# Two hybrid layers walk one written order of steps: chain steps between projection halves, attention in head pairs between inverse levels

## What is computed

```python
h = rmsnorm(x, norm_w)
proj = h @ w_in                      # 1024 x 3752
y_mla  = mla_mixer(m_cq, m_ckv, m_kr, ...) * silu(m_gate)      # 4 heads, causal attention
y_gdn  = gdn_mixer(g_q, g_k, g_v, g_z, g_b, g_a, ...)          # conv, l2norm, gated delta rule
y_moba = moba_mixer(c_q, c_k, c_v, t5_table) * silu(c_gate)    # 4 heads, causal attention
return x + concatenate([y_mla, y_gdn, y_moba]) @ w_out
```

## Time and profile before

| | us |
|---|---|
| median of 3 runs | 2756.01 (2755.51 to 2759.61) |
| the profiled execution, its own time | 2757.31 |
| its span | 2755.5 |
| PE, DVE, ACT, POOL busy in the span | 2437.0, 1251.7, 951.5, 24.8 |
| granted TensorE clock, mean | 0.931 |
| first product of the first hybrid layer | 2130.8 |
| first output product of that layer | 2404.7 |
| the same two of the second layer | 2440.7 and 2711.5 |

### The profile page before, as it was taken

How to read it: one execution, slowest core, us unless ns; L and a number is a source line. 1 busy time by engine, 2 the same in 40 slices (tenths; PEclk the granted TensorE clock), 3 DMA queues, 4 the chain that set the end, 5 groups by cost and what they waited for, 6 DMA issues and landing times.

```text
span 2755.5 us, 40784 instructions
## 1 busy us (share of the span) xinstructions
PE 2437.0 (88%) x15118; PEld 2029.1 (74%) x15118; DVE 1251.7 (45%) x1770; ACT 951.5 (35%) x1299; POOL 24.8 (1%) x24
## 2 busy tenths in 40 slices
PE   4999998899879999979999977988997977798776
PEld 3788886777658888858888756767996965688565
DVE  2433235555653223363323363555546555456453
ACT  2333223443443332233332232345544332143312
POOL 0000000000000000000000000000000000000000
PEclk8999999999989999989999988999999977898787
DMA  8453643222125536432345315113564420044000
GB/s 276 152 165 95 187 141 99 89 81 92 47 61 168 171 102 184 124 90 77 91 135 176 107 47 133 62 62 92 160 185 132 151 79 1 1 141 154 1 1 16
DMA packets 396730, 298.03 MB, mean 108 GB/s; under 512 B 10814, under 2 KB 358596, under 8 KB 396484
## 3 DMA queue, kind: packets, MB, share of 16 engines
q1 hardware_dynamic: 364372, 231.46, 28.9%
q10 hardware_dynamic: 32240, 65.01, 6.8%
HBM read 295.38 MB, written 1.06 MB: 108 GB/s over the span
## 4 chain that ended last, share of the span: by engine, by line
PE 74%; DVE 12%; issue 7%; ACT 4%; SPq 1%; DMA 1%; POOL 1%; DVEq 0%; ACTq 0%; POOLq 0%
PE banks L764 21%; PE banks L765 20%; PE banks L766 20%; DVE wl L1813 3%; ACT wh L1362 3%; PE banks L694 2%; PE banks L745 2%; DVE yT L1779 2%; DVE probn L1792 1%; PE banks L730 1%; PE banks L915 1%; PE banks L738 1%; POOL stat L1696 1%; PE banks L936 1%; DVE big L2206 1%
## 5 line engine op out<-in xcount | busy, mean ns | idle before, releaser
L764 PE MATMUL banks<-uR,wh 128*128 128x512 f32 (+1 forms) x2368 | 831.0, 351 | 60.5 <-DVE uR L1779 42.0
L765 PE MATMUL banks<-uR,wh 128*128 128x512 f32 (+1 forms) x2368 | 819.6, 346 | 0.0
L766 PE MATMUL banks<-uR,wl 128*128 128x512 f32 (+1 forms) x2368 | 818.7, 346 | 0.0
L1813 DVE TENSOR_TENSOR wl<-wraw,wh 128x2048 fp32r<-128x2048 f32 (+1 forms) x224 | 488.6, 2181 | 498.3 <-ACTq L1310 496.7
L1362 ACT ACTIVATE wh<-wraw 128x2048 fp32r<-128x2048 f32 (+1 forms) x224 | 409.1, 1826 | 461.3 <-PE banks L766 414.1
L764 PEld LDWEIGHTS banks<-uR,wh 128*128 128x128 f32 x2368 | 457.8, 193 | 127.5 <-issue 74.4
L766 PEld LDWEIGHTS banks<-uR,wl 128*128 128x128 f32 x2368 | 456.7, 193 | 53.1
L765 PEld LDWEIGHTS banks<-uR,wh 128*128 128x128 f32 x2368 | 457.9, 193 | 49.9 <-issue 0.2
L764 PE MATMUL banks<-gR,wh 128*128 128x512 f32 (+1 forms) x704 | 256.8, 365 | 8.9 <-DVEq L1723 8.9
L765 PE MATMUL banks<-gR,wh 128*128 128x512 f32 (+1 forms) x704 | 255.2, 363 | 0.0
L766 PE MATMUL banks<-gR,wl 128*128 128x512 f32 (+1 forms) x704 | 255.1, 362 | 0.0
(11 more groups left out here) (273 smaller groups left out, 2378.6 us busy)
## 6 DMA issues: line engine op xcount, KB each, us to landing
wraw<-in_ffn_w_in SPq DMA_DIRECT2D x176, 512.0 KB, 5.1
ada_buf<-in_ada_w ACTq DMA_DIRECT2D x27, 2048.0 KB, 8.9
wraw<-in_w_in SPq DMA_DIRECT2D x56, 512.0 KB, 4.7
wraw<-in_ffn_w_out SPq DMA_DIRECT2D x64, 384.0 KB, 4.1
wraw<-in_ffn_w_out SPq DMA_DIRECT2D x64, 320.0 KB, 3.6
wraw<-in_da_w_in SPq DMA_DIRECT2D x24, 512.0 KB, 4.6
wraw<-in_na_w_in SPq DMA_DIRECT2D x24, 512.0 KB, 4.6
yT<-in_ada_w ACTq DMA_DIRECT2D x4, 2048.0 KB, 8.2
```

The costliest lines, as they stand in the source:

```text
L764: mm(o, a[0], b[0], start=first, stop=False)
L765: mm(o, a[0], b[1], start=False, stop=False)
L766: return mm(o, a[1], b[0], start=False, stop=last)
L1813: do(V.tensor_tensor(wl[:, s, 0:n], wraw[:, s, 0:n], wh[:, s, 0:n].bitcast(F32), ALU.subtract), w_lo)
```

## The change

`HY_ORDER` is one list of steps that PE, ACT, DVE and POOL all walk in a hybrid layer. Each engine takes from it the steps that concern it, and does them in that order. A block is now two half steps ("W", n, 0) and ("W", n, 1), and chain steps stand between them. The blocks' order in time is 3, 4, 5, 6, 7, 8, 11, 2, 9, 10, 15, 0, 1, 12, 13, 14 (the weights are loaded in that order). Banks of PSUM are given out by `hy_products`: banks 0 and 1 to blocks, a ring of three (2, 3, 4) to the chain, another of three (5, 6, 7) to `mla`; before, blocks and chain turned over four. `mla` and `moba` attention items are pairs of heads (8 items instead of 16), with one maximum over both heads, and their steps stand between the levels of the inverse and the products of the states. Convolution is now two chunks behind each of blocks 3 to 8. Tiles of the chain (`Xm`, `XT`, `Ym`, `LmT`) lie in the unused half of the activation buffer, diagonals alternate between two buffers, and one semaphore per kind of result takes the place of the two counters. The first output block is cut into four parts.

The letters: St statistics, Di and Fd diagonals and spreads, Sc scaling of q and k, S silu and squares, Ge and Gb gates, T transposes of k and v, Cu and Cb cumulative decays, De decays, KK and QK products, Dv vectors, TL and TY transposes of L, Xi first X, L and P the levels, F the products of the states, Fs and Fc statistics and scaling of the output, Ms, Md, Me, Mq, Mk, Mv, Mr, Mp the parts of `mla`, As scores, At transposes and Av values of an item, U and V halves of the output's input, O output blocks.

```diff
+            first = [*w(3), *w(4), ("W", 5, 0), ("S", 0), ("W", 5, 1), ("W", 6, 0), ("St", 0), ("W", 6, 1), ("W", 7, 0), ("S", 1),
+                     ("Di", 0, 0), ("W", 7, 1), ("St", 1), ("W", 8, 0), ("Sc", 0, 0), ("Di", 0, 1), ("W", 8, 1), *w(11), ("Sc", 0, 1),
+                     ("Di", 1, 0), ("W", 2, 0), ("S", 2), ("Ge",), ("Sc", 1, 0), ("Di", 1, 1), ("W", 2, 1), ("Sc", 1, 1), ("Gb",),
+                     ("W", 9, 0), ("T", 4, 0), ("T", 4, 1), ("W", 9, 1), ("T", 8, 0), ("T", 8, 1), ("Cu",), ("W", 10, 0),
+                     ("Cb", 0), ("Cb", 1), ("W", 10, 1), ("W", 15, 0), ("KK", 0), ("W", 15, 1), ("De",), ("KK", 1), ("W", 0, 0), ("QK", 0),
+                     ("Dv",), ("W", 0, 1), ("QK", 1), ("TL", 0), ("W", 1, 0), ("TL", 1), ("TY", 0), ("W", 1, 1), ("TY", 1),
+                     ("Xi", 0), ("W", 12, 0), ("Ms",), ("Xi", 1), ("W", 12, 1), ("Md", 0)]
+            fill = [[("Me", 0), ("Md", 1), ("W", 13, 0)], [("Me", 1), ("W", 13, 1)],
+                    [("Mq", 0), ("W", 14, 0)], [("Mq", 1), ("Mk", 0)],
+                    [("W", 14, 1), ("Mk", 1)], [("Mr", 0), ("Mv", 0)],
+                    [("Mr", 1), ("Mv", 1)], [("Mp",)]]
+            n = 8
+
+            def item(i):
+                return [("As", i + 1)] * (i + 1 < n) + [("At", i)] + [("Av", i - 1)] * (i > 0)
+
+            fill += [[("As", 0)], *[item(i) for i in range(n)], [("Av", n - 1), ("U", 6)], [("V", 6)], [("O", 0, 0, 0)]]
+            levels = [[[("L", m, 0), ("L", m, 1)], [("P", m, 0), ("P", m, 1)]] for m in range(1, LEVELS)]
+            chain = [x for level in levels for x in level]
+            chain += [[("F", i)] for i in range(1, 7)] + [[("Fs",)], [("Fd", 0)], [("Fc", 0), ("Fd", 1)], [("Fc", 1)]]
+            order = first
+            for x in range(max(len(chain), len(fill))):
+                order = order + (chain[x] if x < len(chain) else []) + (fill[x] if x < len(fill) else [])
...
+                        rest_next()
+                        if 3 <= n <= 8:
+                            convolve(2 * (n - 3))
+                            convolve(2 * (n - 3) + 1)
+                            dve.sem_inc(conv_done, 1)
...
+                    elif kind == "As":
+                        i = at_[0]
+                        b, nk = i % 2, items[i]["nk"]
+                        product(hs_full, *tok, 1)
+                        do(V.reduce_max(negm[:, b, 1, :], banks[:, 0:2, 0:nk], AX.X, negate=True), peak_ready)
+                    elif kind == "At":
+                        i = at_[0]
+                        b, nk = i % 2, items[i]["nk"]
+                        dve.wait_ge(hexp_ready, 8 * l + i + 1)
+                        do(V.reciprocal(rsum[:, b, 1, :], rsum[:, b, 0, :]))
+                        for j in range(2):
+                            x = hprob[:, b, j, 0:nk]
+                            do(V.tensor_scalar(x, x, rsum[:, b, 1, j:j + 1], None, ALU.mult), *([hprob_ready] if j else []))
```

More of the change, by code:

```diff
@@ L410, in moba_items @@
+            for p in range(2):
                 for t in range(2):
                     nk = (t + 1) * P
[L412 to L419, removed]
@@ new lines, in hybrid, with take, four @@
+                items = list(hy_items())
+                w = {}
+                def take(*key):
+                    b, before, _ = HP[(l, *key)]
+                    if before:
+                        pe.wait_ge(hb_free[b], before)
+                    return psum[b]
+                def four(key, pairs):
+                    o = take(*key)
+                    for h in range(GH):
+                        parts = pairs(h)
+                        for k, (a, b) in enumerate(parts):
+                            ins = mm(o[:, h * P:h * P + P], a, b, start=(k == 0), stop=(k == len(parts) - 1))
+                    ins.then_inc(hg_full, 1)
@@ L1599, in hybrid, with product @@
-                for k in (2, 4):
-                    step_v()
-                    A_(uR[:, 0, k:k + 2, CTX:T], yc[:, k:k + 2, :], ACT.Copy).then_inc(uh_ready, 1)
-                for b in range(4):
-                    gemm.up()
-                    lead_next()
+                act.wait_ge(v_hyb, tl["vh"].up())
+                items = list(hy_items())
+                def product(full_sem, *key):
+                    b, _, full = HP[(l, *key)]
+                    act.wait_ge(full_sem, full)
+                    return psum[b], hb_free[b]
@@ L2066, in hybrid, with product, by_head, two @@
                 do(V.memset(convin[:, :, 0:PAD], 0.0))
+                items = list(hy_items())
+                def product(full_sem, *key):
+                    b, _, full = HP[(l, *key)]
+                    dve.wait_ge(full_sem, full)
+                    return psum[b], hb_free[b]
+                def by_head(o):
+                    return o.rearrange("p (a n) -> p a n", n=P)
+                def two(o):
+                    return o.rearrange("p (a n) -> p a n", a=2)
                 def convolve(k):
@@ new lines, in statistics, with spread_out @@
+                def statistics(o, free, means):
+                    for a, e, at_, inv, eps in means:
+                        do(V.tensor_scalar(stat[:, 0, a:e], o[:, at_:at_ + e - a], inv, eps, ALU.mult, ALU.add))
+                    dve.sem_inc(free, 1)
+                    dve.sem_inc(var_ready, 1)
+                    tl["root"].up()
+                def spread_out(tok):
+                    a, nt, d = hy_diag(tok)
+                    dve.wait_ge(root_ready, tl["root"].now())
+                    do(V.tensor_tensor(d[:, 0:nt * P].rearrange("p (a n) -> p a n", n=P), rep(ident, nt),
+                                       wide(stat[:, 1, a:a + nt], P), ALU.mult), hd_ready)
```

1196 lines of the change are left out of this document (636 added, 560 removed).

## The result

The changed kernel takes 2769.93 us (median of 5 runs, 2769.43 to 2771.51); its ratio to the kernel before is 1.0048, 95% interval 1.0034 to 1.0063. It is slower by 0.5%, about 14 us. 2729 was predicted, with 2685 to 2760 as the range, so the time lies outside the range and on the other side of the old one. The profiled execution took 2770.25, its span is 2768.5.

What follows compares the result with a forecast made beforehand. PE's work in the block stage and the round trips to DVE or ACT behind it bound the kernel. Per layer 182 + 34 + 18 + 13.5 = 247.5 us; with tails 27.3 us saved in all, so 2729 us, range 2685 to 2760.

Steps and rivals of the forecast that it cites:

- The clock: Time PE loses at the lower clock: start, block 11 and four holes of 4 us and more, 13.5 us per layer.
- holes of 0.3 to 0.9 us: Short PE holes in the inverse were said to cost no clock, since it has them and 0.96.
- The rest of the sum: Per layer besides clock: 182 us PE work, 34 us block-part waits, 18 us inverse-part waits.
- Rival 2: Holes keep PE at the lower clock through the inverse part: +19 us per layer, 2767 us; 12 in 100.
- The list of waits: PE's waits at named steps, walked: 34 us in the block part, 18 us in the inverse part.
- PE's work: PE's products over a hybrid layer, nearly kept and summed at full clock: 182 us.
- The tail: From last state product to first output product: 3.5 us less than the 14.7 us, per layer.
- Everything else in the kernel stays: Outside the hybrid layers' stretches and tails no time was expected to change.
- What would show it: Profile signs: named DVE-released holes, first layer 247 us, inverse-part clock 0.85 or more; wrong if block part under 135 us.
- 0.75 or less: Granted clock in the inverse part that would show the prediction wrong and Rival 2 right.

Runs made afterwards that it cites:

- experiment 7: Changed kernel, on DVE alone: convolution behind q and k diagonals, scaling ahead of next maximum, `mla` diagonals ahead of ("Xi", 1) and block 12's low half; 2701.11 us.
- experiment 4: Changed kernel, on DVE alone: convolution chunks behind the diagonals of q and k, most of these also ahead of a low half; 2749.25 us.
- experiment 5: Changed kernel, on DVE alone: scaling of each attention item ahead of the next item's maximum; 2738.92 us.
- swap_conv_md: Same run as experiment 7: the DVE moves of experiment 4 and experiment 5 plus the `mla` diagonals moved earlier, against the changed kernel; 2701.11 us.
- experiment 6: The DVE moves of experiment 4 and experiment 5 together, against the changed kernel; 2716.09 us.

## Why the prediction was wrong

**The step that failed is "The clock"**, and in it the term for the item part. The prediction took 13.5 us per layer for the start, block 11 and four long holes, and nothing for the seven holes of 1.6 to 1.8 us among the items. It went by holes of 0.3 to 0.9 us that leave 0.96, and stretched that to twice the length. Measured, PE is busy 12.8 us (first layer) and 7.7 us (second) more in the item part than the same instructions take at the full clock (experiment 7), where the sum has nothing.

The rest of the sum held better. Split by its own terms it gives some 147 us for the block part, 54 for the levels and 47 for the item part (P of level 5 and level 6 7.6, states 7, items 20, holes 12), as an estimate. They are 151.0, 55.8 and 59.7 in the first layer, so 13 of the 19.0 us missed lie in the item part, and 154.4, 55.8 and 55.9 in the second (266.1 for 247.5), so 9 of 18.6. In the block part of the first layer work and clock make some 113 by the sum, and PE is busy 113.2.

**Rival 2 came nearest**: it named this place, "the holes keep PE at the lower clock through the inverse part", and gave 2767 for 2769.93. It got 12 in 100. Its size was right partly by chance: it spread a clock of 0.75 over levels and items, where both together have 0.83 (0.93 and 0.74), and idle time and the block part make up the rest. Its premise, that gaps like the items' stood in today's attention, isn't what that stage shows. PE waited there 4.55 us once and 1.67 us once, and otherwise at most 0.7. Two stretches of it, in the kernel before:

```profile
2272.70:2294.30 21.60, 18.10 (x81) 10.62 (x80) 12.97 (x43) 7.77 (x27) 0.00 (x0) 0.96 0.01 2
2294.34:2311.36 17.02, 16.42 (x46) 8.63 (x46) 6.30 (x21) 4.03 (x14) 0.00 (x0) 0.51 0.00 0
```

The first holds the hole of 1.67 us and has 0.96. The second begins behind holes of 0.64 and 0.68 us, has 0.6 us of idle time in all, and stands at the lower level. So the mean of 0.71 was a warning, but not about long gaps, and "holes of 0.3 to 0.9 us cost nothing" was not safe either. The Trainium skill, "TensorE: Matmul & The Clock Gate", Part 1, says that the array is slow unless activity releases it. The runs agree in direction, since work that computes nothing made the kernel 13.6 us faster; the 17 us in which PE was busy at the lower level aren't explained by it.

**The list of waits held.** Predicted, then measured in the first layer: ("Di", 0, 0) 6.2 and 7.77; ("Di", 0, 1) 2.2 and 3.48; ("Di", 1, 0) 8 and 8.39; ("T", 4, 0) 2.2 and 2.49; ("TY", 0) 3.1 and 4.91; ("Md", 0) 6.5 and 5.68; the items 1.6 to 1.8 and 1.66 to 1.91. ("St", 0) was 4.3 and is 2.38. The mechanism, work that is not urgent ahead in DVE's queue, is shown by experiments 4, 5 and 7, each of which changes that queue alone. ("As", 0) was 1.6 and is 2.20. No wait that wasn't named is over 5 us; 1.48 us for ACT in the item part was not on the list (2.40 in the second layer).

**PE's work** of 182 us at full clock can't be read off directly. swap_conv_md is busy 198.6 us in the same three stretches, two of them at 0.85 and 0.97, so 182 can be right, and no run shows it.

**The tail** was taken at 3.5 us less per layer. From the last state product to the end of the output it is 35.7 for 40.6 and 35.6 for 39.2: 4.9 and 3.6 less. Right.

**"Everything else in the kernel stays"** was wrong by 4 us: the first layer starts 1.1 later (2131.90 for 2130.80), and the stretches between the layers and behind the last take 2.3 and 0.8 more.

**What would show it**: the block part over 135 us (151.0) and the holes at the named steps came. "0.75 or less" in the inverse part, the sign that it was wrong, came for the items of the first layer (0.74), not for those of the second (0.85) and not for levels and items together (0.83).

## What to carry to other kernels

When several engines walk one list, its order must be asked for on each engine apart: PE wants the next item's scores between this item's scores and its transposes, and DVE wants this item's scaling ahead of the next item's maximum. One list can't say both, and the swap on DVE alone was worth 31 of 2770 us. Mixing the inverse part paid 37.7 us as written; mixing the blocks cost 16.6, until what can wait (convolution, a low half that is early) was moved in DVE's queue behind what PE waits for next. With three such moves the same change is 2.05% faster than the kernel before rather than 0.5% slower. And price a wait on PE by what the clock does around it as well as by its length. The mean clock of a stage isn't enough for that: the 0.71 of the old attention stage was 0.96 over 22 us and 0.51 over 17. What decides between the two levels stays open here.

## What the runs showed of the hardware

- With idle stretches of 1.66 to 1.91 us, one in some 7 us, the granted clock of a 60 us stretch was 0.74 in the first layer, and 0.85 in the second (1.66 to 2.24 us). With the same stretches cut by products that nobody reads it was 0.94 (0.80 to 1.04 us left) and 1.00 (0.80 to 1.38). With them gone or at most 1.40 us by the swap on DVE (experiments 5 to 7) it was between 0.89 and 1.00, though one stop of 2.4 us for ACT stayed. The level at which the part starts goes with the difference between layers: with first scores of 1.19 or 1.20 us it was 0.74 in the change and 0.89, 0.92 and 0.89 with the swap, with 0.68 us 0.85 and 1.00, 1.00 and 0.96.
- Clock and idle time don't go together everywhere. In the kernel before PE was at 0.51 for 17.0 us, 16.4 of them busy (2294.34 to 2311.36). With the transposes first the item part had 17.2 us idle and 0.83, in the change 13.9 and 0.75. In the block part 15 us less idle time (experiment 4) left the clock at 0.84.
- Where a switch of ACT's table stands between two functions, it costs what its row shows and no more: in the changed kernel a function ends at 2207.33, the load takes 1.28 us from 2207.35, and the next function starts at 2208.64. In the kernel before, behind a function of 1.91 us that ends at 2239.94, the load starts at 2239.96 and the next function at 2241.26. The Trainium skill, "ScalarE: Activation LUTs", What ACT_TABLE_LOAD costs, gives about 2.7 us with a drain; the load agrees, and the drain isn't seen here. The rows:

```profile
2207.13 0.20 ACT L1676 ACTIVATE gs<-galog 128x4 f32<-128x4 f32 x1
2207.35 1.28 ACT L1677 ACT_TABLE_LOAD   x1
2208.64 0.21 ACT L1677 ACTIVATE gs<-gs 128x8 f32<-128x8 f32 x1
```
